# Probabilities turned by plain transposes after scaling, and the delta rule's raw blocks ahead of the last two convolutions

## What is computed

```python
def latent_layer(x, c, k_ctx, v_ctx, s_ctx, lw):
    h = modulate(rms_norm(x, lw["norm1_g"]), sh1, sc1)
    zq, zk, zv, zqkv, zg, zb, za = jnp.split(h @ lw["w_in"], SPLITS, axis=-1)
    q, k, v = na_heads(zq, zk, zv, lw)                 # per-head RMS norm of q and k
    o_na = neighbourhood_attention(q, k, v, k_ctx, v_ctx, lw["na_rpb"])
    gq, gk, gv, gg, gbeta = gdn_inputs(zqkv, zb, za, lw, axial=True)   # conv, silu, L2 norm, rotary
    o_g, _ = gdn_bidirectional(gq, gk, gv, gg, gbeta, s_ctx)
    o_mix = concat(o_na, gdn_output(o_g, zg, lw["gdn_norm_g"]))
    x = x + g1 * (o_mix @ lw["w_out"])
    return x + g2 * hier_moe(modulate(rms_norm(x, lw["norm2_g"]), sh2, sc2), lw)

# in gated_delta_chunked, per head and chunk
a_mat = where(strict, (k * beta) @ k.T * decay, 0)
t_inv = triangular_solve(eye + a_mat, eye)             # the solved blocks
u, w = t_inv @ (v * beta), t_inv @ (k * beta * exp(gc))
```

## Time and profile before

| | us |
|---|---|
| three executions | 1374.74, 1372.54, 1381.22 |
| median | 1374.74 |
| the profiled execution | 1372.78 |
| its span, first to last instruction | 1371.0 |
| TensorE busy | 1256.0 (92%) |
| VectorE busy | 577.2 (42%) |
| ScalarE busy | 310.4 (23%) |

### The profile page before, as it was taken

How to read it: one execution, slowest core, us unless ns; L and a number is a source line. 1 busy time by engine, 2 the same in 40 slices (tenths; PEclk the granted TensorE clock), 3 DMA queues, 4 the chain that set the end, 5 groups by cost and what they waited for, 6 DMA issues and landing times.

```text
span 1371.0 us, 21250 instructions
## 1 busy us (share of the span) xinstructions
PE 1256.0 (92%) x8943; PEld 616.6 (45%) x8943; DVE 577.2 (42%) x1478; ACT 310.4 (23%) x743; POOL 91.3 (7%) x104
## 2 busy tenths in 40 slices
PE   4999996899978999999989999969899699999996
PEld 1565544575553333333346554537556333333332
DVE  1266977464353212121262687945625412121215
ACT  0237412223131010101022661223322210101010
POOL 0020011110010000000021000021000100000001
PEclk9899998899988999999999999979999899999998
...
GB/s 339 187 151 0 62 149 115 269 229 307 295 241 185 339 399 396 400 397 399 271 291 161 0 62 85 83 199 200 185 347 174 199 289 392 397 397 399 395 397 162
DMA packets 172690, 340.86 MB, mean 249 GB/s; under 512 B 34463, under 2 KB 36903, under 8 KB 172583
## 3 DMA queue, kind: packets, MB, share of 16 engines
...
...
## 4 chain that ended last, share of the span: by engine, by line
PE 71%; DVE 13%; DMA 9%; SPq 4%; issue 2%; ACT 1%; POOL 0%; POOLq 0%; DVEq 0%; ACTq 0%
PE bank L513 67%; PE bank L516 4%; DVE ring L1671 3%; DMA ring<-in_moe_w_dram 3%; DVE arena L1671 2%; DMA ring<-in_ada_w_dram 1%; DMA ring<-in_w_in_dram 1%; DVE arena L1679 1%; DVE small L1679 1%; DMA arena<-tok_dram,idx 1%; SPq L1255 1%; DMA raw_dram<-ring 1%; SPq L1202 1%; SPq L1213 1%; DVE x L1679 1%
## 5 line engine op out<-in xcount | busy, mean ns | idle before, releaser
L513 PE MATMUL bank<-ring,arena 128*32 128x512 f32 (+1 forms) x3088 | 469.6, 588 | 4.8 <-ACT arena L1363 2.9
L513 PE MATMUL bank<-arena 128*32 128x512 f32 (+4 forms) x2160 | 377.9, 530 | 28.8 <-DVE arena L1671 21.6
L1363 ACT ACTIVATE arena<-bank 128x512 f32<-128x512 f32 (+3 forms) x320 | 143.1, 479 | 612.6 <-PE bank L516 328.8
L513 PE MATMUL bank<-ring,hT 128*128 128x512 f32 x576 | 254.5, 597 | 2.4 <-DMA ring<-in_w_in_dram 2.4
L513 PEld LDWEIGHTS bank<-ring,arena 128*32 128x32 f32 (+1 forms) x3088 | 139.6, 114 | 223.0 <-issue 223.0
L513 PEld LDWEIGHTS bank<-arena 128*32 128x32 f32 (+3 forms) x2160 | 130.8, 127 | 162.8 <-issue 124.0
L513 PEld LDWEIGHTS bank<-ring,hT 128*128 128x128 f32 x576 | 108.2, 192 | 128.6 <-issue 125.8
L1671 DVE TENSOR_TENSOR hT<-hT,bank 128x512 f32<-128x512 f32 x24 | 16.5, 687 | 335.0 <-PE bank L513 335.0
L513 PE MATMUL bank<-hT,ring 128*128 128x384 f32 x384 | 132.3, 501 | 0.0
L513 PEld LDWEIGHTS bank<-hT,ring 128*128 128x128 f32 x384 | 73.7, 196 | 48.4 <-issue 4.2
L516 PE MATMUL bank<-const,arena 128*128 128x128 f32 x347 | 52.0, 288 | 33.4 <-DMA arena<-tok_dram,idx 19.6
...
## 6 DMA issues: line engine op xcount, KB each, us to landing
...
expert_dram<-arena SPq DMA_DIRECT2D x22, 512.0 KB, 15.9
...
```

What stands on the lines that cost most here:

```text
L513: return nc.tensor.matmul(out, lhsT, rhs, start=start, stop=stop)
L1363: return nc.scalar.activation(out, in_, func, **kw)
```

## The change

- `probs_cols`, `qk_cols` and `gate_rows` transpose with `tr` instead of multiplying with the identity or a diagonal. `flip` is gone from the tables.
- `turns` becomes `normalised`: VectorE scales each job's probabilities in place by the reciprocal sums, two operations a step, each with a signal of its own (`p_ready`).
- The turning about of latent grid rows moves into ScalarE's copies: q of tiles 1 and 2 in `qk_cols`, and attention's output in `attended`, are written through a pattern whose innermost step is negative.
- The raw blocks: the three turns stand together after convolution 9, the three `head_products` follow, and convolutions 10 and 11 come behind them, on all three engines; `blocks_out` stands behind the load of slab (win, 1).
- `qk_norm` takes three tiles at once: three sums (`qk_sums`), one inverse root over 24 columns, then two operations a tile. For k the sums stand inside the substitution, after row 18 (two) and after row 10 (the third and the norm). `qk_cols` come in threes behind their slab.

```diff
--- before.py
+++ after.py
@@ -208,6 +207,16 @@
     return (0, 1 + d, 2 - d)[step]
 
 
+def reversed_rows(ap):
+
+    return ap.rearrange("p h (r c) -> p h r c", c=GRID_W)[:, :, :, ::-1]
+
+
+def grid_rows(ap):
+
+    return ap.rearrange("p h (r c) -> p h r c", c=GRID_W)
+
+
 def flat(a):
 
     return a.rearrange("p h n -> p (h n)")
...
@@ -581,7 +587,7 @@
                             c0 = (2, 5)[which - 1] * KC + 4 * half
                             b = act_bank("gate", l, which, s, half)
                             for q in range(4):
-                                last = mm(b[:, q * P:(q + 1) * P], mods[:, l, c0 + q, s:s + 1].broadcast_to([P, P]), ident)
+                                last = tr(b[:, q * P:(q + 1) * P], mods[:, l, c0 + q, s:s + 1].broadcast_to([P, P]))
                             last.then_inc(for_act, 1)
 
                 def transposed_norm(which, t0, t1, b_act=None):
@@ -614,11 +620,7 @@
 
                 def qk_cols(i, t):
                     pe.wait_ge(zn_ready, 6 * l + 3 * i + t + 1)
-                    b = act_bank("qkT", l, i, t)
-                    for q in range(4):
-                        last = mm(b[:, q * P:(q + 1) * P], (z, z_k)[i][:, t, q * P:(q + 1) * P],
-                                  tab("flip") if i == 0 and t else ident)
-                    last.then_inc(for_act, 1)
+                    tr4(act_bank("qkT", l, i, t), (z, z_k)[i][:, t, :]).then_inc(for_act, 1)
 
                 if l:
                     transposed_norm(1, 0, 1)
@@ -714,25 +716,25 @@
                 head_cols(1)
                 head_products(0)
                 head_cols(2)
-                conv_cols(10)
-                token_major(0, 1)
                 head_products(1)
                 head_products(2)
-                conv_cols(11)
+                token_major(0, 1)
                 token_major(0, 2)
+                conv_cols(10)
                 arrived(pe, "win", l, 1)
                 token_major(1, 0)
+                conv_cols(11)
                 token_major(1, 1)
+                token_major(1, 2)
                 qk_cols(0, 0)
-                token_major(1, 2)
                 qk_cols(0, 1)
+                qk_cols(0, 2)
                 arrived(pe, "win", l, 2)
                 token_major(2, 0)
-                qk_cols(0, 2)
+                token_major(2, 1)
+                token_major(2, 2)
                 qk_cols(1, 0)
-                token_major(2, 1)
                 qk_cols(1, 1)
-                token_major(2, 2)
                 qk_cols(1, 2)
                 pe.wait_ge(past_in, 32 * (l + 1))
                 b = act_bank("past", l)
@@ -754,12 +756,11 @@
 
                 def probs_cols(step):
                     t = STEPS[step][0]
-                    pe.wait_ge(turn_ready, N_STEPS * l + step + 1)
                     for i, (no, heads_) in enumerate(jobs_of(step)):
                         b = act_bank("probs", l, no)
+                        pe.wait_ge(p_ready, 2 * (N_STEPS * l + step) + i + 1)
                         for q in range(2 if t == 0 else 3):
-                            last = mm(b[:, q * P:(q + 1) * P], p_sb[:, (3 * i + q) * P:(3 * i + q + 1) * P],
-                                      (turn_a, turn_b)[q if t == 0 else 0][:, i])
+                            last = tr(b[:, q * P:(q + 1) * P], p_sb[:, (3 * i + q) * P:(3 * i + q + 1) * P])
                         last.then_inc(for_act, 1)
 
@@ -1274,7 +1275,7 @@
                         bias_rows(0)
                         if l == 0:
                             small_weights()
-                    if name == ("win", l, 2):
+                    if name == ("win", l, 1):
                         blocks_out()
                     if i == len(PRE[l]) - N_OUT + 1 - len([a for a in PRE[l][EARLY if l == 0 else 0:] if a[0] == "ada"]):
                         blocks_back()
@@ -1428,13 +1429,16 @@
                         return
                     f((z, z_k)[which][:, t, :], b[:])
                     if j >= 2:
-                        act.wait_ge(zn_ready, 6 * l + j - 1)
+                        act.wait_ge(z_summed, 6 * l + j - 1)
                     f(sq[:, j % 2, :], b[:], ACT.Square).then_inc(act_emptied, 1)
 
                 def qk_cols(which, t):
                     b = filled("qkT", l, which, t)
-                    dst = (qT, kT)[which]
-                    f(dst[:, :, t * P:(t + 1) * P], b[:].rearrange("p (h n) -> p h n", h=4)).then_inc(act_emptied, 1)
+                    dst, src = (qT, kT)[which][:, :, t * P:(t + 1) * P], b[:].rearrange("p (h n) -> p h n", h=4)
+                    if which == 0 and t:
+                        f(reversed_rows(dst), grid_rows(src)).then_inc(act_emptied, 1)
+                    else:
+                        f(dst, src).then_inc(act_emptied, 1)
 
 
 
...
@@ -1533,7 +1535,11 @@
 
                 def attended(t):
                     act.wait_ge(pv_done, N_STEPS * l + [s for s in range(N_STEPS) if STEPS[s][0] == t][-1] + 1)
-                    f(hT[:, 0:4, t * P:(t + 1) * P], bank[7][:].rearrange("p (k n) -> p k n", k=4)).then_inc(o_na_ready, 1)
+                    dst, src = hT[:, 0:4, t * P:(t + 1) * P], bank[7][:].rearrange("p (k n) -> p k n", k=4)
+                    if t:
+                        f(reversed_rows(dst), grid_rows(src)).then_inc(o_na_ready, 1)
+                    else:
+                        f(dst, src).then_inc(o_na_ready, 1)
 
                 def mixed_T(name, t, k0):
                     b = filled(name, l, t)
...
@@ -1884,7 +1892,7 @@
                         gate_sums()
                     if 2 <= c < 8:
                         decay_rows(c - 2)
-                    if 6 <= c < 12:
+                    if 6 <= c:
                         decay_masks(c - 6)
                     if c == 9:
                         head_lengths()
@@ -1892,19 +1900,23 @@
                         dve.wait_ge(act_emptied, job["conv_back", l, 7])
                         lengths_and_turn(0)
                         lengths_and_turn(1)
-                    if c == 10:
                         lengths_and_turn(2)
-
-                def qk_norm(j):
-                    which, t = divmod(j, 3)
-                    dst = (z, z_k)[which][:, t, :]
-                    dst3 = dst.rearrange("p (h n) -> p h n", h=HEADS)
+                decay_masks(4)
+                decay_masks(5)
+
+                def qk_sums(which, t):
                     dve.wait_ge(act_emptied, job["win", l, which, t])
-                    link(vec.reduce_sum(hss[:, j % 2, :], sq[:, j % 2, :].rearrange("p (h n) -> p h n", h=HEADS), AX))
-                    inverse_root(hr[:, j % 2, :], hss[:, j % 2, :], 1.0 / HD)
-                    link(tt(dst3, dst3, over(hr[:, j % 2, :], HD)))
-                    stt(dst3, dst3, (HD ** -0.5, 1.0)[which], heads(head_g[:, l, which, :], HEADS),
-                        ALU.mult, ALU.mult).then_inc(zn_ready, 1)
+                    vec.reduce_sum(hss[:, t, :], sq[:, (3 * which + t) % 2, :].rearrange("p (h n) -> p h n", h=HEADS),
+                                   AX).then_inc(z_summed, 1)
+                    dve.wait_ge(z_summed, n(z_summed))
+
+                def qk_norm(which):
+                    inverse_root(flat(hr), flat(hss), 1.0 / HD)
+                    for t in range(TILES):
+                        dst3 = (z, z_k)[which][:, t, :].rearrange("p (h n) -> p h n", h=HEADS)
+                        link(tt(dst3, dst3, over(hr[:, t, :], HD)))
+                        stt(dst3, dst3, (HD ** -0.5, 1.0)[which], heads(head_g[:, l, which, :], HEADS),
+                            ALU.mult, ALU.mult).then_inc(zn_ready, 1)
 
                 def head_products(t):
                     for pair in range(2):
@@ -1938,20 +1950,26 @@
                         link(tt(part, v3[:, 0:j, j:j + 1].broadcast_to([n_rows, j, m]),
                                 v3[:, j:j + 1, j + 1:BLOCK].broadcast_to([n_rows, j, m])))
                         link(tt(below, below, part, ALU.add))
-                        if j in (BLOCK - 2, BLOCK - 14, BLOCK // 2 - 8):
-                            qk_norm(3 + (BLOCK - 2, BLOCK - 14, BLOCK // 2 - 8).index(j))
+                        if j == BLOCK - 14:
+                            qk_sums(1, 0)
+                            qk_sums(1, 1)
+                        if j == BLOCK - 22:
+                            qk_sums(1, 2)
+                            qk_norm(1)
                     vec.tensor_copy(t3_, v3.rearrange("p j i -> p i j")).then_inc(solved, 1)
 
                 dve.wait_ge(gexp_ready, l + 1)
                 if l == 0:
                     dve.wait_ge(weights_in, 16 * N_SMALL)
                 head_products(0)
-                qk_norm(0)
                 head_products(1)
                 vec.memset(sub_v[32:64], 0.0)
                 head_products(2)
-                qk_norm(1)
-                qk_norm(2)
+                convolve(10)
+                convolve(11)
+                for t in range(TILES):
```

(15 more changed lines are left out.)

44 lines of the change are left out of this document (20 added, 24 removed).

## The result

The changed kernel takes 1356.08 us (median of 4 runs, 1354.90 to 1357.12), beside 1374.03 for the kernel before: ratio 0.9848, 95% interval 0.9823 to 0.9872. That is 18 us faster where 30 were forecast; the time lies inside the range of 8 in 10 (1333 to 1359), outside the 1336 to 1352 of the forecast itself, and beside the rival "the steps give it back" (1357). The profiled execution took 1354.9 us with a span of 1353.1.

A forecast was written before the change was run, and what follows sets the result against it. TensorE was taken to bound the attention steps, with waits for VectorE and slab DMA ahead of them. Layer 0's 14.2 plus layer 1's 15.9, together 30 us off 1372.8, gave 1343, stated as 1344; 8-in-10 range 1333 to 1359.

The forecast's parts named there:

- the steps give it back: Rival: attention steps' chain or slab stream takes over as TensorE shortens; only 15.8 us stay, 1357; chance 0.22.
- A transposition is one record: TensorE: f32 product leaves two records, transposition one; 0.11 us saved each, 224 in all, 24.6 us of work.
- The rival that it costs as a product: Rival on TensorE: the 24.6 us go, about 10 us from the order remain, 1363; chance 0.06.
- The rival that transposes keep it down: Rival: transposes hold TensorE's clock low in the steps; 1401 if half that work runs slow; chance 0.04.
- Earlier blocks: Raw blocks to first maxima: substitution 184.7 to 217.6, maxima 5.0 us earlier in layer 0, 4.85 in layer 1.
- The chain to step 2, 3.75 us: Attention steps 0 to 2: shorter scaling waits and transposes of probabilities gain 3.75 us per layer.
- Steps 3 to 8 at 0.67: Later attention steps: six transposes each save 0.67 us; layer 0 keeps 3.3 (steps 3 to 7), layer 1 4.0.
- Slab (0,6), 7.6 us: Layer 0, SyncE's queue: solved blocks reached 8.2 us earlier, 17.93 + 12.47 us following as before; 7.6 taken, product near 251.
- The last slabs of layer 0: Layer 0, step 8: its gain goes into the wait for slab (0,10), where TensorE already stood 2.73 us.
- Gates: First residual: 1.8 us per layer, 2.2 with layer 0's step 9; expert gates: 1.1 in layer 0, 1.0 in layer 1.
- Layer 1 without a slab's wait: Layer 1: 8 slabs instead of 12, no slab wait, so its terms sum to 15.9 us.
- The experts' stage moves as a whole.: Experts' stage hangs on TensorE and what it frees; an earlier start moves it as a whole.

The follow-up runs named there:

- e1: Kernel before plus transposes, normalised probabilities and reversed writes, in the old order of raw blocks, convolutions, norms and SyncE's queue; ratio 0.9939.
- e2: Changed kernel with the transposes of q, k, probabilities and gates turned back into products with the identity; ratio 0.9956.
- e3: Changed kernel with the second score job's bank claimed only ahead of that job's product; ratio 0.9836 to the kernel before.
- e5: Changed kernel with the store of the solved blocks ahead of the load of slab (0,5) on SyncE; ratio 0.9886 to the kernel before.
- e6: Changed kernel with SyncE's load of slab (0,6) ahead of the second half of the bias rows; ratio 0.9865 to the kernel before.
- e10: Changed kernel; in layer 1 SyncE holds the load of slab (1,6) until the solved blocks' small products are done; 1354.33 us, ratio 0.9807.
- e11: Changed kernel with modulation products between probabilities and scores, and layer 1's load of slab (1,6) held; 1362.23 us, ratio 0.9868.
- e4: Kernel before with the second score job's bank claimed only ahead of that job's product; ratio 1.0009.
- e12: The changed kernel itself, unedited, run again on the chip of the later runs; 1358.28 us, ratio 0.9846.
- e8: Changed kernel with four edits: banks one by one, store first, bias rows later, four of layer 0's modulation products a half step earlier; ratio 0.9917.

## Why the prediction was right or wrong

- **A transposition is one record.** Right. There are 224 records fewer, the 16 gates take 1.97 us instead of 3.82, and TensorE's busy time fell by 25.6 us (24.6 counted; the busy time of one kernel differs by 3 to 6 us between profiles). The rival that it costs as a product is gone.
- **The clock.** The rival that transposes keep it down is gone for the steps: from 262 to 322 us the granted clock is 1.00. The Trainium skill (TensorE: Matmul & The Clock Gate, "Part 4: PE-mode transpose") has transposes not count for the clock gate; with 0.9 us of them in steps of 8 us or more this trace neither bears that out nor refutes it. In small the clock did take something, behind waits of TensorE: product (0,4), behind waits of 4.15 and 1.79 us, took 3.37 us instead of 1.92 (granted clock 0.56), and the latent expert gates of layer 1 with the transposes ahead of them take 3.3 us from start to start instead of 2.8 (granted clock 0.53, before 1.00), with a new wait of 0.99 us for VectorE some 6 us ahead. The prediction's reading for this rival, "after 6 us without work", is not in its rows: ahead of 258.37 TensorE waited 1.23 us, and behind the wait of 6.16 us at 232.16 the product at 243.45 ran at full clock.
- **Earlier blocks.** Right within 1.1 us for the third raw tile, both ends of the substitution and the first maxima, and 4.8 us of lead are gained from layer 1's start to its first probabilities (8.9 to 13.8), as forecast. The way of the raw blocks through DRAM was over-sized: their load goes out 4.5 us behind the store (166.84 and 171.35) instead of 9.2, which changes nothing, since VectorE works until 183.62 without them. A q sum is waited for (2.10 us at 176.17), which stood among the signs of being wrong; it costs nothing at that end.
- **The chain to step 2, 3.75 us.** Right in layer 1: 3.76 from the first probabilities to the small products behind those of step 2 (13.75 to 17.51). In layer 0 it is 3.2, as product (0,4) ran at the low clock. That step 1 gave its part is luck: the scalings and GpSimd's keys were left open, and they missed each other by 1.3 us. In e1 and e2 they meet, and TensorE waits 1.3 and 1.4 us longer there.
- **Steps 3 to 8 at 0.67.** Mis-sized. From the transposes to the next work it was 2.51 us and is 2.13: 0.38 a step, 0.38 to 0.40 in layer 1. The prediction gave the shorter transposes to the path and overlooked that a bank stands between them and the scores. That is 0.29 less in some eleven steps, 3.2 us; e3 shows that the wait goes when the bank is claimed later, and that then the scores stand one after the other. In layer 1 it does not show in the sum: the steps still gain 4.6 us up to the gates (4.5 forecast), because the kernel before had stopped there once more (1.01 us at 934.81, "issue") and the changed one did not.
- **Slab (0,6), 7.6 us.** Mis-sized: 5.1, of which 1.0 had been there since layer 0's first token product. The step that failed is "17.93 + 12.47 us then follow as before": the 17.93 became 21.69, since the store stands behind the load of (0,5), its reads follow 9.57 us behind it instead of 6.38, and the bias rows took 6.99 us to issue instead of 5.29. "A crowded queue may cost some" was right, the size (0.6) was not. The product came at 253.25, later than the 253 named as a sign of being wrong. e5 and e6 show that no order of these issues that was tried helps.
- **The last slabs of layer 0.** Right in kind: step 8's gain went into the wait seen at 325.50 before. The slab named there is (1,2), the eleventh of the twelve, not (0,10); the row is the same.
- **Gates.** 1.8 us came at layer 0's step 9 and first gates (2.2 forecast), 1.85 at layer 1's. At the expert gates 0.9 came in layer 0, and the gathered tokens behind them took 0.7 of it back; in layer 1 the lead fell by 0.9 (22.0 to 21.0), for the low clock named above and for the gathered tokens.
- **Layer 1 without a slab's wait.** Right, but the stop for instructions was not foreseen: 3.30 us against 0.27. With the product behind it the lead falls from 17.5 to 15.6. e10 and e11 show that it hangs on the slab load. How much of it belongs to the change is less sure: the stop is 1.33 us in e4, whose order is that of the kernel before, and 2.06 in e12. The fixed waits of that layer, 2.41 us for ScalarE and 4.99 for VectorE ahead of its last turned outputs, are as before.
- **"The experts' stage moves as a whole."** Not in this pair of profiles. The lead falls by 0.7 us from layer 0's first gathered tokens to layer 1's start, by 1.0 in layer 1's experts and by 2.2 from the last batches to the end; in the first and the last of these stretches TensorE stands for 1.01 us at 684.52 and 1.89 at 1337.83, both "issue". But these two stops are no mark of the change: e4, with the old order, has them (1.04 and 2.16 us), and e5 to e8, with the new one and all on one chip, have neither. No instruction packet stands 2 to 3 us ahead of either. Their cause stays open.
- **The number.** 1356 lies beside the first rival's 1357 by luck. That rival had nothing left but 7.9 us a layer; in fact the chain and part of the steps stayed, and other losses took their place.

Sum of the misses by the leads, against 30.1 us forecast and 17.9 seen in the spans: slab (0,6) 2.5, layer 0's steps and first gates 1.2, the stop in layer 1 less what the chain gave 1.9, the expert gates with the gathered tokens 2.9, the experts' stages 3.8.
